# A Mamba-2, gMLP and MLP decoder step: combining y in two pieces, Silus ahead of y's squares, and GpSimd's state loads in mid-step

## What is computed

```python
xbc_act = jax.nn.silu(conv)                      # depthwise causal convolution of x, B, C, 4 taps
# prompt: chunked scan, 8 groups of 4 heads, chunks of 128
y_diag = einsum('bcgrqs,bcsgrp->bcqgrp', cb * decay, xdt)
y_off = einsum('bcqgn,bcgrpn,bcqgr->bcqgrp', Cc, h_prev, exp(a_cum))
# samples: one step of h = exp(dt*A) * h + dt * B x^T, y = C h
y = y + xs * d_skip[:, None]
y = y.reshape(b, l, D_INNER) * jax.nn.silu(z)
yg = y.reshape(b, l, SSD_GROUPS, D_INNER // SSD_GROUPS)
yg = yg * lax.rsqrt(jnp.mean(yg * yg, axis=-1, keepdims=True) + RMS_EPS)
return (yg * norm_g) @ w_out, new_conv, new_ssm
```

## Time and profile before

| | us |
|---|---|
| median of three runs | 1620.63 |
| the profiled execution | 1624.18 |
| its span in the profile | 1622.40 |
| TensorE busy in the span | 1516.0 (93%) |
| VectorE busy | 1161.5 (72%) |
| ScalarE busy | 685.9 (42%) |
| GpSimd busy | 586.5 (36%) |

### The profile page before, as it was taken

One profiled execution on the slowest core, in us unless ns is written; L12 is line 12 of the kernel. 1 busy time (PEld: TensorE's weight loads), 2 busy tenths in 40 slices (PEclk: granted clock), 3 DMA queues, 4 the chain that ended last, 5 costly groups with the idle time before them and its releaser, 6 DMA issues.

```text
span 1622.4 us, 30561 instructions
## 1 busy us (share of the span) xinstructions
PE 1516.0 (93%) x12329; PEld 1493.6 (92%) x12329; DVE 1161.5 (72%) x1533; ACT 685.9 (42%) x1043; POOL 586.5 (36%) x573
## 2 busy tenths in 40 slices
PE   5898889879996899999999999999999999999996
PEld 5898878879886889999999999999999999999996
DVE  4688888773888788979798454364454897979944
ACT  3755645624556253434343343342234343434321
POOL 3067676641776532324165122200001141404801
PEclk9999999999998999999999999999999999999998
DMA  5444455343443422423324232313222323242311
GB/s 166 109 141 142 133 151 167 127 144 102 137 144 118 139 74 79 131 79 105 105 79 130 79 104 82 102 55 105 79 79 79 105 79 105 79 130 79 126 57 53
DMA packets 158931, 173.44 MB, mean 107 GB/s; under 512 B 13912, under 2 KB 146896, under 8 KB 158784
## 3 DMA queue, kind: packets, MB, share of 16 engines
q1 hardware_dynamic: 137032, 131.30, 25.7%
q0 software_dynamic: 9472, 26.50, 5.2%
q10 hardware_dynamic: 12288, 13.71, 2.9%
HBM read 159.53 MB, written 12.21 MB: 106 GB/s over the span
## 4 chain that ended last, share of the span: by engine, by line
PE 63%; DVE 1%; issue 1%; ACT 1%; POOL 0%; ACTq 0%; DVEq 0%
PE ps L941 28%; PE ps L662 17%; PE ps L966 15%; PE ps L1048 1%; PE ps L682 1%; DVE rstd L1806 0%; PE ps L1016 0%; DVE w_lo L2111 0%; PE ps L919 0%; PE ps L705 0%; POOL ssum L1595 0%; ACT arena L1539 0%; ACT w_hi L1434 0%; PE ps L770 0%; PE ps L1040 0%
## 5 line engine op out<-in xcount | busy, mean ns | idle before, releaser
L662 PE MATMUL ps<-h_hi,w_hi 128*128 128x260 f32 (+2 forms) x1296 | 274.4, 294 | 9.3 <-issue 4.7
L662 PE MATMUL ps<-h_lo,w_hi 128*128 128x260 f32 (+2 forms) x1296 | 265.0, 287 | 0.0
L662 PE MATMUL ps<-h_hi,w_lo 128*128 128x260 f32 (+2 forms) x1296 | 264.3, 286 | 0.0
L1434 ACT ACTIVATE w_hi<-w 128x512 fp32r<-128x512 f32 x232 | 138.2, 626 | 242.6 <-PE ps L941 163.3
L662 PEld LDWEIGHTS ps<-h_hi,w_hi 128*128 128x128 f32 x1296 | 206.1, 193 | 12.5 <-issue 10.3
L941 PE MATMUL ps<-h_hi,w_hi 128*128 128x260 f32 x1024 | 207.2, 284 | 4.7 <-DVE work L2143 4.5
L941 PE MATMUL ps<-h_hi,w_lo 128*128 128x260 f32 x1024 | 207.1, 284 | 0.0
L941 PE MATMUL ps<-h_lo,w_hi 128*128 128x260 f32 x1024 | 206.6, 283 | 0.0
L2111 DVE TENSOR_TENSOR w_lo<-w,w_hi 128x512 fp32r<-128x512 f32 x232 | 188.2, 838 | 25.4 <-ACT w_hi L1434 24.9
L662 PEld LDWEIGHTS ps<-h_lo,w_hi 128*128 128x128 f32 x1296 | 204.9, 193 | 0.0
L662 PEld LDWEIGHTS ps<-h_hi,w_lo 128*128 128x128 f32 x1296 | 204.3, 192 | 0.0
(11 more groups left out here) (259 smaller groups left out, 3592.8 us busy)
## 6 DMA issues: line engine op xcount, KB each, us to landing
w<-in_mlp_w_up SPq DMA_DIRECT2D x32, 1024.0 KB, 5.4
w<-in_mlp_w_down SPq DMA_DIRECT2D x32, 1024.0 KB, 5.2
w<-in_ssd_w_in SPq DMA_DIRECT2D x16, 1024.0 KB, 6.6
w<-in_cm_w_in SPq DMA_DIRECT2D x16, 1024.0 KB, 5.4
w<-in_ssd_w_in SPq DMA_DIRECT2D x16, 512.0 KB, 5.5
arena<-in_state_ssm POOLq DMA_DIRECT2D x64, 128.0 KB, 3.5
arena<-scr_a ACTq DMA_DIRECT2D x16, 512.0 KB, 3.8
arena<-scr_bc POOLq DMA_DIRECT2D x32, 256.0 KB, 3.8
```

The source lines that it names most:

```text
L662: mm = pe.matmul(ps[:, 2 * slot + b, 0:tn], w[:, pair.w_slot, k, col:col + P], x[:, k, t0:t0 + tn], start=(k == 0 and n == 0), stop=(k == ...
L1434: nc.scalar.activation(blocks(w_hi)[:, (p.ring + n) % 8], src, ACT.Copy)\
```

## The change

VectorE's `combine` becomes two functions. `combine_prompt(g)` holds the two multiplies by the decay and the two sums, and runs ahead of `conv(nxt, 3)`; `combine(g)` keeps the skip terms of the samples and the gates, behind `sample(g, 3)`. `evac_unit(nxt, 3)` moves from behind `sample(g, 2)` to behind `states(g)`. On ScalarE `y_squares(g - 1)` moves behind the two Silus of x, and `abc_load(g, 0)` waits for the four operations of `combine_prompt` and no longer for the gates. On GpSimd `load_bc(n + 1)` and `load_states(n + 1)` move from the end of a step to behind its multiply by the decay. All is computed as before.

```diff
--- before.py
+++ after.py
@@ -1262,8 +1262,8 @@
             def abc_load(g, i):
 
                 if i == 0:
-                    if due(2 * g):
-                        act_e.wait_ge(comb_done, 2 * g)
+                    if due(6 * g - 2):
+                        act_e.wait_ge(cchain, 6 * g - 2)
                 elif due(2 * g):
                     act_e.wait_ge(ydiag_done, 2 * g)
                 act_e.dma_start(abc[:, i], scr_a[4 * g + 2 * i:4 * g + 2 * i + 2, :].partition_broadcast(P))\
@@ -1303,10 +1303,10 @@
                 more = nxt < GROUPS
                 split_w(Pair(group_pair(g, 2) + 1))
                 exp_m(g, 1)
-                y_squares(g - 1)
                 abc_load(g, 0)
                 silu(g, 2)
                 silu(g, 3)
+                y_squares(g - 1)
                 cst(g)
                 act_e.wait_ge(bc_tr, g + 1)
                 if due(16 * g):
@@ -1650,6 +1650,10 @@
                                             state.rearrange("p (i b) n -> p i b n", i=2),
                                             dtf[:, 2 * g:2 * g + 2, 8 + b0:10 + b0].unsqueeze(3).broadcast_to([P, 2, 2, N]),
                                             ALU.mult).then_inc(decay_done, 1)
+                    if n % 4 in (1, 2):
+                        load_bc(n + 1)
+                    if n % 4 and n + 1 < 4 * GROUPS:
+                        load_states(n + 1)
                     pool.wait_ge(bcs_landed[n % 2], 16 * (n // 2 + 1))
                     pool.wait_ge(decay_done, n + 1)
                     for i in range(2):
@@ -1667,10 +1671,6 @@
                         pool.dma_start(dst, state[:, 2 * i:2 * i + 2, :]).then_inc(sstored[n % 2], 16)
                     if n % 4 == 0 and g < GROUPS - 1:
                         y_low(g - 1)
-                    if n % 4 in (1, 2):
-                        load_bc(n + 1)
-                    if n % 4 and n + 1 < 4 * GROUPS:
-                        load_states(n + 1)
 
             for g in range(GROUPS):
                 window(g)
@@ -1944,24 +1944,30 @@
                     dve.wait_ge(hchain, 3 * g + c)
                     nc.vector.tensor_tensor(hprev[:, c, :], hprev[:, c, :], bank, ALU.add).then_inc(hstep_done, 1)
 
-            def combine(g):
-
+            def combine_prompt(g):
+
+                n = 6 * g
                 for i in range(2):
-                    n = 3 * (2 * g + i)
                     dve.wait_ge(yoff_done, 2 * g + i + 1)
                     dve.wait_ge(ef_done, 2 * g + i + 1)
                     nc.vector.tensor_tensor(abc[:, 0, i, CH:TP], ps[:, 5 + i, CH:TP], abc[:, 0, i, CH:TP], ALU.mult)\
                       .then_inc(cchain, 1)
-                    if i == 0:
-                        dve.wait_ge(sred_done, 4 * g + 4)
+                for i in range(2):
+                    dve.wait_ge(cchain, n + i + 1)
+                    dve.wait_ge(y1_done, 2 * g + i + 1)
+                    nc.vector.tensor_tensor(work[:, i, CH:TP], work[:, i, CH:TP], abc[:, 0, i, CH:TP], ALU.add)\
+                      .then_inc(cchain, 1)
+
+            def combine(g):
+
+                n = 6 * g + 4
+                dve.wait_ge(sred_done, 4 * g + 4)
+                for i in range(2):
                     nc.vector.scalar_tensor_tensor(out=work[:, i, TP:T], in0=act[:, g % 2, 2 + i, S0:CONV_N:TAPS],
                                                    scalar=dtf[:, 2 * g + i, 16:17], in1=ysmp[:, i, :],
                                                    op0=ALU.mult, op1=ALU.add).then_inc(cchain, 1)
-                    dve.wait_ge(cchain, n + 1)
-                    dve.wait_ge(y1_done, 2 * g + i + 1)
-                    nc.vector.tensor_tensor(work[:, i, CH:TP], work[:, i, CH:TP], abc[:, 0, i, CH:TP], ALU.add)\
-                      .then_inc(cchain, 1)
-                    dve.wait_ge(cchain, n + 3)
+                for i in range(2):
+                    dve.wait_ge(cchain, n + i + 1)
                     dve.wait_ge(z_silu_done, 2 * g + i + 1)
                     nc.vector.tensor_tensor(work[:, i, :], work[:, i, :], zs[:, i, :], ALU.mult)\
                       .then_inc(comb_done, 1)
@@ -2023,10 +2029,11 @@
                 if g == 0:
                     dve.wait_ge(cdec_landed, 16)
                 states(g)
+                evac_unit(nxt, 3)
                 if more:
                     conv(nxt, 2)
                 sample(g, 2)
-                evac_unit(nxt, 3)
+                combine_prompt(g)
                 if more:
                     conv(nxt, 3)
                 sample(g, 3)
```

## The result

The changed kernel took **1628.0 us** (median of five runs, 1627.37 to 1629.17) where the kernel before took 1620.2 on the same chip (five runs, 1618.96 to 1620.99). The ratio is 1.0041 with a 95% interval of 1.0029 to 1.0052: slower, by about 7 us. The forecast was 1604.4, faster, and the measured time is outside its range.

What follows compares the result with a forecast made beforehand. It took the ring from combine through y_sum and GpSimd's four steps back to combine as the bound. Gains 3.0 (group 0) + 10.2 (groups 1 to 6) - 0.5 (group 5) + 3.5 (group 7) = 16.2 us off 1620.63: 1604.4, range 1593 to 1616.

Steps and rivals of the forecast that it cites:

- Part 1, combine in two: VectorE: four operations of combine move ahead of the last convolution, covered by its wait for GpSimd; 2.0 us less each turn.
- The stall of line 781: TensorE's 33.9 us wait for combine's first multiply: would go, with small waits at line 816 instead.
- Part 2, y_squares: ScalarE: squares behind two Silus let the norm come earlier; 0.7 us a turn at GpSimd's y_low, bounds 0 and 1.5.
- Part 3, smul_done: GpSimd, step 1's loads wait until VectorE has multiplied sample(g, 0), at 155.5 in group 1: a wait of 3.5 us.
- Part 3, step 1 beside the split: GpSimd's step 1 work, 4.0 us, now falls beside VectorE's weight split: 0.9 us added, bounds 0 and 1.5.
- Part 3, the stores: GpSimd's mid-step loads wait for stores landing 2.2 us after issue: 0.3 us in steps 2 and 3, up to some 4.6.
- group 0: First window: a load wait of 5.2 and two us of combine go; gain 2.1 to 4.6 us, taken as 3.0.
- The walk of group 1: GpSimd's and VectorE's steps summed through group 1: combine ends at 183.1 instead of 184.29, parts 1 and 3 gaining 1.2 us.
- group 7: Last window, no loads before its last sums and no convolutions: a gain of 3.5 us.
- C: Rival: GpSimd's queue stops at smul_done and later steps start from there; each turn 1 us longer, 1626 to 1630; 6%.
- B: Rival: new waits (step 1 +0.6, late stores +0.6 twice) take what combine gives; about 1619 us; 8%.
- The list of what would show it wrong: Step 1's sums over 5.5 us, stores holding L1621 over 1 us, or VectorE waiting for nothing at sample(g, 3).

Runs made afterwards that it cites:

- combine alone: The changed kernel with GpSimd's loads put back to the end of a step, two-piece combine and ScalarE's order kept: 0.9888 of the kernel before, 1606.7 us.
- control: Two-piece combine with GpSimd's loads at the end of a step, unedited, rerun on the chip of the later-broadcast and later-split runs: 0.9911 of the kernel before, 1607.3 us.

## Why the prediction was wrong

Point by point, in its own steps:

- **Part 1, combine in two: right.** Forecast 2.0 us a turn; combine alone gave 52.63 for 54.67 in the first and 1.8 on the mean of six. The cover held: `sample(g, 3)` waits 2.13 us in the changed kernel, and the last convolution ends 2.1 us before the sums do, as forecast. The stall of line 781 became one at line 816, but a large one (40.2).
- **Part 2, y_squares: not to be told from nothing.** The pair of `y_low` took 2.76 us, not 4.04, but GpSimd reached it 0.9 us later in the turn (at 148.31 for 146.93, with the turn's start 0.5 later), so its end gained 0.4 us.
- **Part 3, smul_done: right.** `sample(1, 0)` was multiplied at 155.57 (forecast 155.5), the stop was 3.80 (3.5), and against load waits it is worth nothing either way.
- **Part 3, step 1 beside the split: mis-sized.** I added 0.9 to 4.0 us of work, with 0 and 1.5 as bounds; its sums took 6.1 (157.90 to 163.98). The outer product took 2.65 where the shortest take 0.61: 2.04 of the 2.29 us of the split. That is 1.2 over the forecast and outside its bounds, which came from `y_low` beside a split. I had set its loss of 1.46 us against the whole split of 2.28, but the two overlapped for only 1.62 us (146.93 to 148.55). Read so, the loss is the overlap less some 0.15 us, and it is that in the later rows too: 2.04 of 2.19 in the changed kernel, 2.10 of 2.25 in the decay, 1.87 of 2.02 in the outer product of step 2. The rule of the Trainium skill ("SBUF — State Buffer", Who interferes with whom) that I had weighed and set aside, that the two block each other fully, is close to what the trace shows here; with it the forecast would have been 1612.8, still faster.
- **Part 3, the stores: the step that failed most.** I gave 0.3 us to the wait in step 2; it was 2.42. The landing was taken at the median of the earlier trace rows, 2.2. The row also had 6.7 as its longest, and I named it without asking what made it long. The runs showed that it is 4.18 for the store that meets the broadcast. The restart of 0.53 us I didn't have at all; it accounts for step 3's wait of 0.93 against 0.5. In group 0, where I expected to gain 3.0, the state loads waited 2.00 and 2.67 for stores, and 0.5 was lost:

```profile
101.67 1.41 POOL L1621 DMA_DIRECT2D arena<-in_state_ssm  x2 [2.00 <-DMA out<-arena]
...
113.23 1.42 POOL L1621 DMA_DIRECT2D arena<-in_state_ssm  x2 [2.67 <-DMA out<-arena]
```

The landings behind these two waits, from the chain of waits:

```profile
94.08 7.01 DMA out<-arena
...
108.23 4.06 DMA out<-arena
```

The first is the store with the 6.7 of the earlier trace rows: step 0 of group 0, issued just behind two 512 KB weight loads of SyncE and beside four 128 KB loads of ScalarE, in both kernels. Before the change nothing waited for it. Which of these loads makes it long is not shown. The second met a broadcast issued 0.07 us ahead of it.

The walk of group 1 closes with these: start of the loads 0.4 late, sums of step 1 +1.2, store +2.1, step 3's wait +0.4, its sums -0.6 (3.4 for 4.0). That is 3.5, and `combine` ended at 186.68 where I had 183.1. Against combine alone the stage gives the same picture: GpSimd's decays, outer products and sums took 157.5 us and there 149.4 (37.3, 51.7 and 60.4), 8.1 for the split; the waits ahead of L1621 were 25.7 and with the broadcast out of the way 12.2, 13.5 for the meeting, and that run was 13 us faster by the medians (16 to 18 by the ratios). What is left of the waits, 28.9 and 12.2, with 1.47 in each of seven windows for the loads now ahead of the last sums, is 51.4 against 50.4 of load waits: next to nothing. That the 8.1 is the split's is supported by the run with loads at the end and the split later, 7.6 us slower than its control. Over the stage the ends of `combine` say: groups 1 to 6 gained 9.7 in the sum and lost 9.5; group 0 lost 0.5 for a gain of 3.0; group 7 gained 7.2, 3.7 more than forecast. That makes 19.0 of the 23.6 us between 1604.4 and 1628.0. Most of the rest is that I took the difference off the median of the runs, while the profiled execution of before was 3.6 us above it and that of after (1627.4) 0.6 below its own.

**The rivals.** C had the sign and the price (1626 to 1630) with half the mechanism: the steps behind the stop did lose to the split, but 1.2 of the 3.5 us. The larger half was B's, the stores, which I had priced at 0.6. Each was weighed as if alone, and they are not: the stop and the split put step 1's stores some 8 us later (from 156.4 to 164.27), just beside a broadcast that had stood clear of both stores before. The list of what would show it wrong held: step 1's sums over 5.5 us, and stores holding L1621 for over 1.

## What to carry to other kernels

When a change moves a queue's work, list the transfers of the other queues that it now meets, with their sizes, and price its own at the length they have beside those: a median landing comes from where they met nothing. An engine's idle time can be cover for another one's memory traffic: here the weight split lay beside the issue of loads and the 2.8 us wait for them and cost nobody anything, and once the wait was gone it lay on GpSimd's work, at about 2 us a turn. And when two edits cure the same symptom, run both together before giving each a price.

## What the runs showed of the hardware

- A store of 128 KB from GpSimd's queue to DRAM landed 2.2 us behind its issue, and 4.18 with a 512 KB broadcast issued 0.07 us ahead of it on ScalarE's queue (3.8 and 3.9 with the broadcast 0.02 us ahead of two stores). A 1 MB weight load alone did not do this. State loads of 128 KB landed after 4.6 to 4.9 us beside the broadcast, after 3.4 to 3.6 without it, and GpSimd waited 1.4 us longer for them.
- Between a store's landing and the issue of GpSimd's load that waited for it lay 0.53 us in the rows above, and 0.90 once in group 0.
- VectorE's split (2.3 us, two inputs in SBUF) stretched whichever compute instruction of GpSimd it met by nearly the time that the two overlapped: an outer product from 0.61 to 2.65 and from 0.62 to 2.49, a decay from 1.05 to 3.15. The split itself took 2.29 us in the first of these, 2.51 and 2.68 in the two others. GpSimd's issues of DMAs were not stretched beside it: two state loads took 1.43 us beside the split in the control, and 1.41 to 1.48 in the other rows.
